# Bias rows of a two-layer transformer kernel written by GpSimd, entry by entry, instead of by three matmuls

## The chip, the cores and the metric

One NeuronCore of one Trainium2 chip. The metric is the device time of one execution in microseconds, the median of several. Engines are named as in the profile: PE is TensorE (its matmuls; PEld its weight loads), DVE is VectorE, ACT is ScalarE, POOL is GpSimd, SP is SyncE. A name with q behind it is that engine's queue of DMA issues.

## The reference

Two transformer blocks on one sequence of 512 tokens and 16 meta tokens, width 1024. What matters here is the first block's position bias. A table `rel_bias` of 32 buckets by 16 heads holds it: the first 8 columns serve attention A (a sliding window), the last 8 attention B (top-k latent attention). The bias of a query and a key depends on their distance alone:

```python
def t5_bucket(dist):
    max_exact = N_BUCKETS // 2
    d = jnp.maximum(dist, 1).astype(jnp.float32)
    large = max_exact + (jnp.log(d / max_exact) / math.log(MAX_DISTANCE / max_exact)
                         * (N_BUCKETS - max_exact)).astype(jnp.int32)
    large = jnp.minimum(large, N_BUCKETS - 1)
    return jnp.where(dist < max_exact, dist, large)
...
    bias = bias_table[t5_bucket(jnp.maximum(dist, 0))]
    s = jnp.where(allowed[None, :, None, None], s + bias.astype(jnp.float32)[None], NEG)
```

Around it stand the input product with `w_in` (1024 to several thousand columns, cut into queries, keys, values and gates), the two attentions, their output products, a gated feed-forward of width 2816, and then a second block of the same size.

## The kernel before

The kernel is written engine by engine: each engine has its own program, and semaphores join them. The order on each engine is the order in which its program is written; no scheduler moves anything. Weights come in slices of 1024 rows by 128 columns through two buffers, b = 0 and 1. For each slice SP issues the load into `stage` (`load`, L589), ACT rounds it to the high half `wh` (L918), DVE or POOL subtracts to get the low half `wl` (L1398 on DVE), and PE runs `product` (L2273): three matmuls for each 128 rows, of which the first waits for `lo[b]` (the low half is there) and for `ev[b]` (the result before it on this buffer has been taken out of PSUM). DVE takes results out, for the keys by `take_keys` (L1549), which multiplies them by `Rk`, the spread inverse norm of each token.

The change lies in the first 50 us. There the phases follow one another as `kv1` (four slices, in pairs 0 and 1: keys and values of both attentions), `bq1` (two slices), `iq1` (two), `aq1` (four). At that place the kernel before does this:

- SP loads the table into `tab` (33 partitions, one a bucket, the last a row of -1e30 set by POOL at L719) and two tables of zeros and ones, `hotA` (33 by 383) and `hotB` (33 by 655), which say for each distance which bucket it falls into (L633 to L635).
- PE, after pair 0 of `kv1`, spreads the inverse norms (`spread_first`, L2433: a small matmul for the meta tokens and one of 512 columns, L2365), then multiplies `tab` by the tables (L2443 to L2445). The results are two rows for each of 8 heads, the bias by distance. They lie in `psL` and `psT`. Then it goes on with pair 1 of `kv1`.
- ACT takes the spread norms out into `Rk` (L976), and DVE takes the meta part (L1522, L1523). When both are there, DVE takes out pair 0 (`bkvT`, `ikwT`), runs a dozen small operations (`start_rest`, L1526), copies the bias rows from PSUM into `fA` and `fB` (L1541 to L1544), and then makes the low half of pair 1's second slice.
- POOL waits for `fA_ok`, writes the two rows to DRAM (L786, L787), fans row A out to 128 copies in DRAM (L777), and reads them back, each partition one element further on, as the bias tile `biasA` (L783). Then it waits for `key_taken` (L792) and goes on with other work. Row B follows the same way much later, inside the loop of the gates (L796 to L801). The scores of attention A use `biasA` at L1697.

`fA` and `fB` lie in the same memory as the input tile `xin`.

Of the kernel before, what the change touches and what calls it, by code (L numbers as in the profile page):

```python
# [29 lines left out]
P = 128  # L30
# [4 lines left out]
NB = SEQ // P  # L35
# [8 lines left out]
NH = 8  # L44
EPS = 1e-6
NEG = -1e30
# [3 lines left out]
BUCKETS = 32  # L50
# [14 lines left out]
def bucket(dist):  # L65

    exact = BUCKETS // 2
    d = np.maximum(dist, 1).astype(np.float32)
    span = np.float32(np.log(128 / exact))
    large = exact + (np.log(d / np.float32(exact)) / span * np.float32(BUCKETS - exact)).astype(np.int32)  # L70
    return np.where(dist < exact, dist, np.minimum(large, BUCKETS - 1))


# [228 lines left out]
def build(nc, t, out):  # L302
    with ExitStack() as ctx:
# [8 lines left out]
        def at(name, shape, offset, dt=F32):  # L312

            n = int(np.prod(shape[1:])) * size[dt]
            assert offset + n <= nc.sbuf_usable_end, (name, offset + n - nc.sbuf_usable_end)
            return nc.alloc_sbuf_tensor_at(name, shape, dt, offset=offset), -(-(offset + n) // 32) * 32

        def keep(name, shape, dt=F32):
            tensor, top[0] = at(name, shape, top[0], dt)
            return tensor  # L320
# [18 lines left out]
        nsink = keep("nsink", [P, 2, NH])  # L339
        tab = keep("tab", [BUCKETS + 1, 2 * NH])  # L340
        wuv = keep("wuv", [P, NH * HD])
# [85 lines left out]
        sqacc, _ = at("sqacc", [P, 2, SEQ], tail)  # L427
        hotA, o5 = at("hotA", [BUCKETS + 1, LEN_A], tail)
        hotB, o5 = at("hotB", [BUCKETS + 1, LEN_B], o5)
        assert o5 <= o  # L430
        fA, o7 = at("fA", [NH, LEN_A], gate0)
# [85 lines left out]
        def last_bank(half, b):  # L517
# [27 lines left out]
            sem(n) for n in "consts zeros gvec_t gvec_ok x_t x_high xT_act xT_dve xlo x_sq meta_t metaT_ok mhi mlo".split()]  # L545
        f_mm, fA_ok, f_row, f_out, biasA_in, biasB_in = [sem(n) for n in "f_mm fA_ok f_row f_out biasA_in biasB_in".split()]
        diag_ok, bcast, R_ok, ssq_in, ssq_mm = [
# [40 lines left out]
        def _(sp):  # L588
# [43 lines left out]
            load("kv1", 0, 1, win1, kv_cols[1])  # L632
            sp.dma_start(tab[0:BUCKETS, :], t["rel_bias"]).then_inc(tab_in, 16)  # L633
            sp.dma_start(hotA[:], t["hot_a"]).then_inc(tab_in, 16)
            sp.dma_start(hotB[:], t["hot_b"]).then_inc(tab_in, 16)  # L635
            for n in range(2, 4):
# [71 lines left out]
        def _(pool):  # L708
# [9 lines left out]
                                        pattern=[[META, NH]], channel_multiplier=-1))  # L718
            own.link(pool.memset(tab[BUCKETS:BUCKETS + 1, :], NEG))  # L719
            own.link(pool.memset(st[:, 0, 0:6], 1.0))  # L720
# [58 lines left out]
            def windows(dram, length, tile_, width, h0, h1, signal):  # L779
# [3 lines left out]
                pool.dma_start(tile_[:, h0:h1, :], src).then_inc(signal, 16)  # L783

            pool.wait_ge(fA_ok, 2)
            pool.dma_start(fA_row[:], fA[:]).then_inc(f_row, 16)  # L786
# [598 lines left out]
        def _(v):  # L1385
# [140 lines left out]
            def start_rest():  # L1526

                b0 = ROW["b_gates"]
                g = ROW["subln_gain_2"]
                dv.link(v.tensor_scalar(subg[:], gvec[:, g:g + 1], 1.0 - LAMBDA0, None, ALU.mult))  # L1530
                g1, g2 = ROW["final_norm_g"], ROW["norm_mix_2"]
                dv.link(v.tensor_tensor(g12[:], gvec[:, g1:g1 + KD], gvec[:, g2:g2 + KD], ALU.mult))
                dv.link(v.tensor_scalar(bhalf[:], gvec[:, b0:b0 + 2 * KD], 0.5, None, ALU.mult))
                v.wait_ge(lam_in, 64)
                dv.link(v.tensor_tensor_reduce(out=lamj[:], in0=lam4[:, 0, :], in1=lam4[:, 1, :], scale=1.0, scalar=0.0,
                                               op0=ALU.mult, op1=ALU.add, accum_out=lam[:, 0:1]))
                dv.link(v.tensor_tensor_reduce(out=lamj[:], in0=lam4[:, 2, :], in1=lam4[:, 3, :], scale=1.0, scalar=0.0,
                                               op0=ALU.mult, op1=ALU.add, accum_out=lam[:, 1:2]))
                v.memset(lamj[:, 0:1], 0.0).then_inc(lam_sum, 1)
                v.wait_ge(f_mm, 1)  # L1540
                v.tensor_copy(fA[:], psL[0:NH, 0, 0:LEN_A]).then_inc(fA_ok, 1)  # L1541
                v.wait_ge(f_mm, 2)
                v.tensor_copy(fB[:, 0:512], psL[0:NH, 1, :])
                v.tensor_copy(fB[:, 512:LEN_B], psT[0:NH, 0, 0:LEN_B - 512]).then_inc(fA_ok, 1)  # L1544

# [726 lines left out]
        def _(pe):  # L2272
# [167 lines left out]
            spread_first()  # L2440
            pe.wait_ge(tab_in, 48)
            pe.wait_ge(xT_act, 6)
            pe.matmul(psL[0:NH, 0, 0:LEN_A], tab[:, 0:NH], hotA[:], start=True, stop=True).then_inc(f_mm, 1)  # L2443
            pe.matmul(psL[0:NH, 1, :], tab[:, NH:2 * NH], hotB[:, 0:512], start=True, stop=True)
            pe.matmul(psT[0:NH, 0, 0:LEN_B - 512], tab[:, NH:2 * NH], hotB[:, 512:LEN_B], start=True, stop=True).then_inc(f_mm, 1)  # L2445
            products("kv1", hn, first=1, meta=1)
            pe.wait_ge(fA_ok, 2)
            products("bq1", hn)
# [476 lines left out]
```

## Time and profile before

| | us |
|---|---|
| median of 3 runs | 1473.24 |
| lowest and highest | 1470.36, 1475.11 |
| profiled execution | 1473.38 |
| its span in the trace | 1471.7 |

The profiled execution takes 1.7 us more than its span, for what lies around it. The span begins at 0.00 in all the rows below. Mean granted clock of PE: 0.997 of full speed.

A row of the timeline gives start, duration, engine, line, operation, output and inputs; in square brackets stands the time for which the engine had been idle and who released it. A group of instructions that run into one another shows them as one row with their count, from the first start to the last end.

### The profile page before, as it was taken

The page shows a single profiled execution, that of the slowest core. Times are in us where ns is not written, and L with a number is a line of the kernel's source. Part 1 is how long each engine was busy: PE and PEld are TensorE (multiplying, and loading weights), DVE is VectorE, ACT ScalarE, POOL GpSimd, SP SyncE. Part 2 cuts the span into 40 slices and gives each one's busy share as a digit, 9 for nine tenths or more (in the row PEclk, how much of TensorE's full clock was granted, in tenths as well). Part 3 has the DMA queues.
Part 4 walks back from the last instruction along what each step waited for, and adds up shares of the span by engine and source line. Part 5 has one row for each costly group of instructions (what it writes and reads, how often), then busy time and mean ns, then how long its engine had stood idle before and what let it go on. Part 6 is the DMA issues. An engine that isn't in the chain of part 4 may idle for free.

```text
span 1471.7 us, 23871 instructions
## 1 busy us (share of the span) xinstructions
PE 1452.7 (99%) x8712; PEld 1253.2 (85%) x8712; DVE 975.2 (66%) x1779; ACT 654.3 (44%) x1175; POOL 258.2 (18%) x260
## 2 busy tenths in 40 slices
PE   9999999999999999999999999999999999999998
PEld 8868786888898898999899777777888988989997
DVE  6678977575776576787744372434767765867875
ACT  5234446535453353465411373544344533534643
POOL 2024536201101100000003675331011001000000
PEclk9999999999999999999999999999999999999999
DMA  7536674249899993663223237653388999736632
GB/s 187 148 100 211 173 133 130 79 111 191 202 328 226 250 217 98 199 184 106 86 86 86 58 101 162 151 188 80 107 186 226 305 218 242 213 95 195 185 104 93
DMA packets 342909, 236.91 MB, mean 161 GB/s; under 512 B 24729, under 2 KB 322837, under 8 KB 342814
## 3 DMA queue, kind: packets, MB, share of 16 engines
q1 hardware_dynamic: 305518, 152.24, 36.4%
q0 software_dynamic: 37216, 83.27, 24.8%
q8 instruction: 60, 0.98, 0.3%
q14 instruction: 35, 0.29, 0.1%
q10 hardware_dynamic: 80, 0.14, 0.0%
HBM read 233.48 MB, written 81.88 MB: 214 GB/s over the span
## 4 chain that ended last, share of the span: by engine, by line
PE 88%; DMA 6%; DVE 3%; ACT 1%; issue 1%; DVEq 0%; SPq 0%; POOL 0%; ACTq 0%
PE psL L2293 37%; PE psL L2520 12%; PE psS L2316 10%; PE psL L2316 6%; PE psS L2293 5%; PE psT L2316 4%; PE psT L2529 2%; DMA stage<-in_w_ffn_up 1%; DMA stage<-in_w_ffn_gate 1%; DMA stage<-in_w_ff_up 1%; PE psL L2655 1%; PE psS L2836 1%; PE psS L2570 1%; PE psL L2791 1%; PE psS L2814 1%
## 5 line engine op out<-in xcount | busy, mean ns | idle before, releaser
L918 ACT ACTIVATE wh<-stage 128x1024 fp32r<-128x1024 f32 (+3 forms) x211 | 203.6, 965 | 362.1 <-PE psL L2293 199.6
L1398 DVE TENSOR_TENSOR wl<-stage,wh 128x1024 fp32r<-128x1024 f32 (+2 forms) x168 | 183.8, 1094 | 57.7 <-ACT wh L918 57.3
L2293 PE MATMUL psL<-hid,wh 128*128 128x512 f32 x672 | 207.3, 390 | 0.0
L2520 PE MATMUL psL<-hn,wh 128*128 128x512 f32 x496 | 165.0, 414 | 0.8 <-DVE yn L2176 0.8
L2293 PE MATMUL psL<-hn,wh 128*128 128x512 f32 x528 | 165.0, 394 | 0.0
L2293 PEld LDWEIGHTS psL<-hid,wh 128*128 128x128 f32 x672 | 125.6, 188 | 26.2 <-DVE wl L1398 0.6
L2293 PE MATMUL psL<-hid,wl 128*128 128x512 f32 x336 | 130.7, 389 | 0.0
L746 POOL TENSOR_TENSOR wl<-stage,wh 128x1024 fp32r<-128x1024 f32 (+1 forms) x43 | 97.7, 2273 | 172.7 <-ACT wh L918 172.7
L2293 PEld LDWEIGHTS psL<-hn,wh 128*128 128x128 f32 x528 | 97.7, 188 | 23.1 <-issue 3.3
L2520 PEld LDWEIGHTS psL<-hn,wh 128*128 128x128 f32 x496 | 84.5, 189 | 24.5 <-issue 11.1
L2293 PE MATMUL psL<-hn,wl 128*128 128x512 f32 x264 | 102.9, 390 | 0.0
L1901 DVE TENSOR_TENSOR wsl<-wsum,wsh 128x1024 fp32r<-128x1024 f32 x72 | 88.2, 1224 | 22.3 <-ACT wsh L1166 21.4
L2520 PE MATMUL psL<-hn,wl 128*128 128x512 f32 x248 | 97.8, 394 | 0.0
L2316 PE MATMUL psS<-xt,wsh 128*128 128x256 f32 x432 | 80.2, 283 | 0.8 <-ACT part_x L1226 0.8
L2293 PE MATMUL psL<-mix,wh 128*128 128x512 f32 x256 | 79.9, 393 | 0.8 <-DVE wl L1814 0.8
L2293 PE MATMUL psS<-hn,wh 128*128 128x264 f32 x416 | 78.5, 290 | 0.9 <-DVE hn L1845 0.5
L1166 ACT ACTIVATE wsh<-wsum 128x1024 fp32r<-128x1024 f32 x72 | 75.4, 1048 | 5.6 <-DMA wsum<-weight_sums_1g 1.9
L2293 PEld LDWEIGHTS psL<-hid,wl 128*128 128x128 f32 x336 | 63.1, 188 | 13.2
L2028 DVE TENSOR_TENSOR ft<-psL,Rk 128x512 f32<-128x512 f32 x46 | 31.8, 691 | 62.4 <-PE psL L2293 62.4
L2316 PEld LDWEIGHTS psS<-xt,wsh 128*128 128x128 f32 x432 | 67.4, 192 | 1.0 <-ACT part_x L1226 1.0
L2293 PEld LDWEIGHTS psS<-hn,wh 128*128 128x128 f32 x416 | 65.7, 192 | 2.6 <-issue 1.2
L2316 PE MATMUL psS<-xt,wsl 128*128 128x256 f32 x216 | 61.1, 283 | 0.0
(507 smaller groups left out, 3333.0 us busy)
## 6 DMA issues: line engine op xcount, KB each, us to landing
stage<-in_w_in SPq DMA_DIRECT2D x53, 512.0 KB, 4.0
wsum<-weight_sums_1g SPq DMA_DIRECT2D x18, 512.0 KB, 5.2
wsum<-weight_sums_1u SPq DMA_DIRECT2D x18, 512.0 KB, 5.3
wsum<-weight_sums_2g SPq DMA_DIRECT2D x18, 512.0 KB, 4.7
wsum<-weight_sums_2u SPq DMA_DIRECT2D x18, 512.0 KB, 4.5
stage<-in_w_out SPq DMA_DIRECT2D x16, 512.0 KB, 4.7
stage<-in_w_ffn_down SPq DMA_DIRECT2D x32, 256.0 KB, 3.0
stage<-in_w_ff_down SPq DMA_DIRECT2D x32, 256.0 KB, 3.0
```

Source lines behind the costliest of these rows:

```text
L746: pool.tensor_tensor(wl[:, b, 0:n], stage[:, b, 0:n], wh[:, b, 0:n].bitcast(F32), ALU.subtract).then_inc(lo[b], 1)
L918: act.activation(wh[:, b, 0:n], stage[:, b, 0:n], ACT.Copy).then_inc(hi[b], 1)
L1166: act.activation(wsh[:, cols], wsum[:, cols], ACT.Copy).then_inc(ws_hi, 1)
L1398: v.tensor_tensor(wl[:, b, 0:n], stage[:, b, 0:n], wh[:, b, 0:n].bitcast(F32), ALU.subtract).then_inc(lo[b], 1)
L1901: v.tensor_tensor(wsl[:, cols], wsum[:, cols], wsh[:, cols].bitcast(F32), ALU.subtract).then_inc(ws_lo, 1)
L2028: v.tensor_tensor(ft[:, 2 * b, :], psL[:, b, :], R, ALU.mult).then_inc(upper_ok, 1)
L2293: ins = pe.matmul(dst, w[:, b, k * P:(k + 1) * P], x[:, part, k, c0:c1], start=done_ + n == 0, stop=done_ == kc - 1 and n == 2)
L2316: ins = pe.matmul(dst, w[:, cols], x(part, k), start=not add and k + n == 0, stop=k == KD // 2 - 1 and n == 2, skip_group_check=True)
L2520: ins = pe.matmul(psL[:, b, :], w[:, b, k * P:(k + 1) * P], hn[:, part_, k, META:], start=k + n == 0, stop=k == KD - 1 and n == 2)
L2529: ins = pe.transpose(psT[:, n % 2, m * P:(m + 1) * P], tile[:, col:col + P], ident[:])
L2570: ins = pe.matmul(psS[:, 2 * (i % 2) + 1, h * HD:(h + 1) * HD], PTa[:, u % 2, n * P:(n + 1) * P], avn[:, c, h // 4 * HD:h // 4 * HD + HD], ...
L2655: ins = pe.matmul(psL[:, i % 2, h * HD:(h + 1) * HD], PT[:, n % 4, m * P:(m + 1) * P], vB[:, c, h * HD:(h + 1) * HD], start=h == 0 and m = ...
```

## The change

The three matmuls, the two tables of zeros and ones, the row of -1e30 in `tab`, DVE's three copies and the semaphore `f_mm` go. The table is now loaded with heads on partitions (`tabT`, 8 partitions by 2 by 32), by two DMAs of SP that read it element by element. POOL writes `fA` and `fB` itself: for each run of distances with one bucket, a copy of that bucket's entry, broadcast over the run (`bucket_runs`); where no key is allowed, a memset to -1e30. Row A has 34 runs, 32 of them copies, and row B 33, also with 32 copies. Of these 64 copies 63 are of 1 to 15 elements and one is of 415. The third new thing is POOL's three waits ahead of them: for the table, for the squares of x and for DVE's `diag_ok`, since `fA` lies on `xin`. PE no longer waits for `fA_ok` ahead of `bq1`.

```diff
+def bucket_runs(length, far):
+
+    dist = (length - P) - np.arange(length)
+    which = np.where((dist < 0) | (dist >= far), BUCKETS, bucket(dist))
+    edges = [0, *(np.flatnonzero(np.diff(which)) + 1).tolist(), length]
+    return [(int(which[x0]), x0, x1) for x0, x1 in zip(edges[:-1], edges[1:])]
...
-        tab = keep("tab", [BUCKETS + 1, 2 * NH])
+        tabT = keep("tabT", [NH, 2, BUCKETS])
...
-            sp.dma_start(tab[0:BUCKETS, :], t["rel_bias"]).then_inc(tab_in, 16)
-            sp.dma_start(hotA[:], t["hot_a"]).then_inc(tab_in, 16)
-            sp.dma_start(hotB[:], t["hot_b"]).then_inc(tab_in, 16)
+            for n in range(2):
+                sp.dma_start(tabT[:, n, :], t["rel_bias"][:, n * NH:(n + 1) * NH].rearrange("b h -> h b"), allow_slow_non_contiguous=True).then_inc(tab_in, 16)
...
-            own.link(pool.memset(tab[BUCKETS:BUCKETS + 1, :], NEG))
...
+            pool.wait_ge(tab_in, 32)
+            pool.wait_ge(x_sq, NB - 1)
+            pool.wait_ge(diag_ok, 1)
+            for n, (row, length, far) in enumerate(((fA, LEN_A, P), (fB, LEN_B, 1 << 20))):
+                for b, x0, x1 in bucket_runs(length, far):
+                    if b == BUCKETS:
+                        ins = pool.memset(row[:, x0:x1], NEG)
+                    else:
+                        ins = pool.tensor_copy(row[:, x0:x1], tabT[:, n, b:b + 1].broadcast_to([NH, x1 - x0]))
+                ins.then_inc(fA_ok, 1)
             pool.wait_ge(fA_ok, 2)
...
-                v.wait_ge(f_mm, 1)
-                v.tensor_copy(fA[:], psL[0:NH, 0, 0:LEN_A]).then_inc(fA_ok, 1)
-                v.wait_ge(f_mm, 2)
-                v.tensor_copy(fB[:, 0:512], psL[0:NH, 1, :])
-                v.tensor_copy(fB[:, 512:LEN_B], psT[0:NH, 0, 0:LEN_B - 512]).then_inc(fA_ok, 1)
...
-            pe.wait_ge(tab_in, 48)
             pe.wait_ge(xT_act, 6)
-            pe.matmul(psL[0:NH, 0, 0:LEN_A], tab[:, 0:NH], hotA[:], start=True, stop=True).then_inc(f_mm, 1)
-            pe.matmul(psL[0:NH, 1, :], tab[:, NH:2 * NH], hotB[:, 0:512], start=True, stop=True)
-            pe.matmul(psT[0:NH, 0, 0:LEN_B - 512], tab[:, NH:2 * NH], hotB[:, 512:LEN_B], start=True, stop=True).then_inc(f_mm, 1)
             products("kv1", hn, first=1, meta=1)
-            pe.wait_ge(fA_ok, 2)
             products("bq1", hn)
```

How the order moves. On PE, between pair 0 and pair 1 of `kv1`, in the kernel before:

```order
L2436 MATMUL psS<-meta_diag,ones 128x32
L2365 MATMUL psT<-diag,ones 128x512
L2443 MATMUL psL<-hotA,tab 8x383
L2444 MATMUL psL<-hotB,tab 8x512
L2445 MATMUL psT<-hotB,tab 8x143
L2293 MATMUL psS<-hn,wh 128x264 x2
L2293 MATMUL psS<-hn,wl 128x264
```

and in the changed kernel (its lines are numbered some 8 higher there):

```order
L2301 MATMUL psS<-hn,wl 128x264
L2444 MATMUL psS<-meta_diag,ones 128x32
L2373 MATMUL psT<-diag,ones 128x512
L2301 MATMUL psS<-hn,wh 128x264 x2
L2301 MATMUL psS<-hn,wl 128x264
```

Pair 1 now stands right behind the spreading of the norms, with nothing between them. On POOL, behind its loads of the small vectors (`lam_86` holds the four lambda vectors), before:

```order
L739 DMA lam_86<-in_lambda_k_2 128x64
L786 DMA bias_row_A<-fA 8x383
L787 DMA bias_row_B<-fB 8x655
L777 DMA bias_by_distance_A<-bias_row_A 1024x1x383
L783 DMA biasA<-bias_by_distance_A 128x8x256
```

and in the changed kernel, where the copies of one element close row A:

```order
L794 MEMSET fA 8x128
L796 COPY fA<-tabT 8x15
L796 COPY fA<-tabT 8x14
...
L796 COPY fA<-tabT 8x1 x16
L794 MEMSET fA 8x127
L796 COPY fB<-tabT 8x415
...
L796 COPY fB<-tabT 8x1 x16
L794 MEMSET fB 8x127
L799 DMA bias_row_A<-fA 8x383
L800 DMA bias_row_B<-fB 8x655
```

67 instructions now stand ahead of the first of POOL's bias DMAs, on the engine that issues them.

## Rows read from the trace of the kernel before

**Rows 1.** The page: busy times; the engines of the chain that ended last.
```profile
PE 1452.7 (99%) x8712; PEld 1253.2 (85%) x8712; DVE 975.2 (66%) x1779; ACT 654.3 (44%) x1175; POOL 258.2 (18%) x260
...
PE 88%; DMA 6%; DVE 3%; ACT 1%; issue 1%; DVEq 0%; SPq 0%; POOL 0%; ACTq 0%
```

**Rows 2.** That chain in order of time: start us, us, what.
```profile
25.43 0.74 PE psL L2443 x2
26.16 0.86 PE psL L2444 x2
27.02 0.24 PE psT L2445 x2
27.27 11.78 PE psS L2293 x96
```

**Rows 3.** Timeline at the place of the change: PE, DVE, ACT.
```profile
27.20 0.51 PE L2293 MATMUL psS<-hn,wh 128*128 128x264 f32 x2
...
23.57 1.20 DVE L1398 TENSOR_TENSOR wl<-stage,wh 128x1024 fp32r<-128x1024 f32 x1
...
26.15 0.71 DVE L1549 TENSOR_TENSOR bkvT<-psS,Rk 128x528 f32<-128x528 f32 x1 [0.41 <-DVE Rmeta L1523]
...
28.55 0.54 DVE L1541 COPY fA<-psL 8x383 f32<-8x383 f32 x1
...
29.84 1.20 DVE L1398 TENSOR_TENSOR wl<-stage,wh 128x1024 fp32r<-128x1024 f32 x1
...
25.46 0.60 ACT L976 ACTIVATE Rk<-psT 128x512 f32<-128x512 f32 x1 [3.96 <-PE psT L2365]
...
50.06 1.06 ACT L918 ACTIVATE wh<-stage 128x1024 fp32r<-128x1024 f32 x1 [4.39 <-PE psL L2293]
```

**Rows 4.** POOL's instructions by line and form: count, busy us, mean ns, idle before.
```profile
L852 POOL COPY m8d<-W 128x16 f32<-128x16 f32 x16 | 3.2, 201 | 16.6 <-DVE W L2168 16.4
...
L861 POOL COPY vm<-vaT 128x512 f32<-128x512 f32 x1 | 1.0, 997 | 34.2 <-DVE vaT L1549 34.2
...
L713 POOL MEMSET lam_mask<- 128x1 f32 x1 | 0.1, 99 | 0.1
```

**Rows 5.** Timeline of POOL: its bias DMAs and what follows.
```profile
30.20 0.54 POOL L786 DMA_DIRECT2D bias_row_A<-fA  x1 [13.28 <-DVE fB L1544]
...
43.14 0.94 POOL L783 DMA_DIRECT2D biasA<-bias_by_distance_A  x1 [9.38 <-DMA bias_by_distance_A<-bias_row_A]
...
77.52 0.29 POOL L793 COPY cm<-cT 128x128 f32<-128x128 f32 x1 [33.44 <-DVE ikz L1624]
```

**Rows 6.** The tile biasA: its user (ns, first and last start), its landing.
```profile
L1697 DVE CUSTOM_DVE_ANT_0 W3a<-psS,biasA,nsink x32: 364/480/485, 107.8 to 209.7; 128x256 f32<-128x256 f32 x24, 128x144 f32<-128x144 f32 x8
...
DMA to landing us min/median/max: 6.0/6.0/6.0
```

**Rows 7.** SP's loads issued at 11.09 and 35.70 (KB, us to landing), and at 41.49.
```profile
stage<-in_w_in SPq DMA_DIRECT2D x1, 512.0 KB, 5.2
...
stage<-in_w_in SPq DMA_DIRECT2D x1, 512.0 KB, 8.6
...
41.49 0.37 SPq L595 DMA_DIRECT2D stage<-in_w_in  x1
```

**Rows 8.** DMA packets, MB, share of 16 engines: windows 54:57, then 16:20.
```profile
q1 hardware_dynamic: 1884, 0.47, 70.9%
...
q0 software_dynamic: 141, 0.15, 103.3%
```

**Rows 9.** PE's longest wait, and 516:520: engines' busy us, PEclk, DMA share, GB/s.
```profile
516.33 0.72 PE L2316 MATMUL psL<-xt,wsh 128*128 128x256 f32 x2 [2.23 <-ACT part_x L1226]
...
516.00:520.00 4.00, 3.67 (x18) 3.68 (x19) 3.90 (x5) 2.80 (x7) 0.00 (x0) 0.57 1.04 175
```

**Rows 10.** Timeline of DVE and POOL side by side in the second layer.
```profile
790.43 2.43 DVE L2113 TENSOR_SCALAR tmp<-dist 128x384 f32<-128x384 f32 x1
...
789.88 2.76 POOL L746 TENSOR_TENSOR wl<-stage,wh 128x1024 fp32r<-128x1024 f32 x1 [3.40 <-ACT wh L918]
```

More of the change, by code:

```diff
@@ L427, in build @@
         sqacc, _ = at("sqacc", [P, 2, SEQ], tail)
-        hotA, o5 = at("hotA", [BUCKETS + 1, LEN_A], tail)
-        hotB, o5 = at("hotB", [BUCKETS + 1, LEN_B], o5)
-        assert o5 <= o
         fA, o7 = at("fA", [NH, LEN_A], gate0)
@@ L545, in build @@
             sem(n) for n in "consts zeros gvec_t gvec_ok x_t x_high xT_act xT_dve xlo x_sq meta_t metaT_ok mhi mlo".split()]
-        f_mm, fA_ok, f_row, f_out, biasA_in, biasB_in = [sem(n) for n in "f_mm fA_ok f_row f_out biasA_in biasB_in".split()]
+        fA_ok, f_row, f_out, biasA_in, biasB_in = [sem(n) for n in "fA_ok f_row f_out biasA_in biasB_in".split()]
         diag_ok, bcast, R_ok, ssq_in, ssq_mm = [
```

## The prediction

> **What bounds the kernel now.** I read the page first: PE is busy for 99% of the span, and 88% of the chain that ended last is PE's [rows 1]. So an edit is worth what it takes off PE, or what it makes PE wait. Then I read that chain in order of time around 25 us, to see whether the removed matmuls are links of it. They are: 0.74, 0.86 and 0.24 us stand between the spreading of the norms and pair 1 of `kv1` [rows 2]. Third comes the timeline of the other engines at the same place, to see what PE would wait for if it came there earlier, and last POOL's idle time and the loads, for what the new work could push.
>
> **Removed from PE: 1.84 us, of which 0.3 count.** The three matmuls are 0.74 + 0.86 + 0.24 = 1.84 us of the chain [rows 2]. Without them PE is ready for pair 1 at 25.43. But the first slice of pair 1 writes the PSUM bank that `bkvT` is taken from (`ev[0]` in `product`), and `bkvT` is on DVE from 26.15 to 26.86 [rows 3]. It can't be earlier: it needs `Rk` from ACT, 25.46 to 26.06, and that is released by the spreading matmul [rows 3], which keeps its time. So the matmuls ran under a chain PE, ACT, DVE that is nearly as long as they are. PE starts pair 1 some 0.05 us behind DVE's end, at 26.91, where it started at 27.20 [rows 3]: 0.29 us gained, and some 1.5 us of new idle time. The other input of that slice, its low half, is ready at 23.57 + 1.20 = 24.77 [rows 3], before that. The price is bounded by 0, if DVE is held up by a few tenths, and by the whole 1.84. I take 0.29, because the row that sets it stands unchanged.
>
> **Removed from DVE: nothing on the path.** The three copies fill 28.55 to 29.84. Behind them waits the low half of pair 1's second slice, ready at 29.84 + 1.20 = 31.04 [rows 3]. PE's two slices of pair 1 are 11.78 us together [rows 2], so it comes to the second at 27.27 + 5.89 = 33.16. There were 2.1 us of slack. Now the low half is ready at 28.55 + 1.20 = 29.75 and PE comes at 32.9: 3.1 us. The wait of `bq1` for `fA_ok` was met at 30.1, long before PE came to it at 39.05, the end of pair 1 [rows 2]; its removal is worth nothing.
>
> **Added to POOL: 67 instructions, some 11 us, hidden.** They can start when DVE's `diag` is done, about where the next instruction begins, 23.57 [rows 3]. The trace has no copy of 8 partitions by 1 to 15. The nearest is one of 16 elements with 201 ns, and the cheapest POOL instruction of all is a memset with 99 ns [rows 4]. The copy of 512 elements takes 997 ns [rows 4], so 415 elements are 201 + (415 - 16) x (997 - 201) / (512 - 16) = 841 ns. With 63 short copies and three memsets the ends are 66 x 0.099 + 0.84 = 7.4 us and 66 x 0.201 + 0.84 = 14.1 us. I take 0.15 each, between the two, since instructions that run into one another overlap a little: 66 x 0.15 + 0.84 = 10.7 us. The rows are ready at 34.3 (31.0 to 37.7). POOL issued the first bias DMA at 30.20 [rows 5], so the chain of bias A moves back by 4.1 us (0.8 to 7.5). It ended with an issue at 43.14 [rows 5] and a landing 6.0 later, at 49.1, and its user starts at 107.8 [rows 6]. Now it ends at 53.2 (at most 56.6). POOL's next work is at 77.52 [rows 5], 33.4 us behind its last issue. Both covers hold unless each of the 66 costs over 0.6 us, three times the dearest row.
>
> **Moved: the big DMAs of bias A.** The fan-out to DRAM lay between 33 and 43 and moves to some 37 to 47; it is behind no queue of SP's, but it shares the 16 DMA engines. The load of a weight slice issued at 35.70 ran beside it and took 8.6 us [rows 7]. That load now gets shorter. The next, at 41.49 [rows 7], gets into it: at 8.6 us it lands at 49.8 after an issue at 41.2. ACT rounds that slice at 50.06 [rows 3], at 49.8 in the changed kernel. So it lands just in time. PE wants the slice only behind `iq1`'s first product, seven us later. Cost: 0, at most a few tenths on ACT that PE never sees.
>
> **Added to SP: 512 single elements in place of three small tables.** The table now comes in 2 x 8 x 32 runs of 4 bytes, on the same queue ahead of the load issued at 11.09, which landed at 11.09 + 5.2 = 16.3 [rows 7]. The nearest hardware-made small packets are 1884 of 256 bytes, which filled 0.709 x 16 x 3 us = 34 us of engine time, 18 ns each [rows 8]. The dear end is a stretch of software-made ones, reading short vectors again and again: 1.033 x 16 x 4 = 66 us for 0.15 MB, that is 590 runs of 256 bytes at 0.11 us [rows 8]. Spread over all 16 engines, 32 runs each, they delay the load by 0.6 to 3.6 us; on 8 of them, a head each, by 1.2 to 7.2. The load may land so late that rounding (1.06) and low half (1.20) [rows 3] still end by 25.5, when DVE turns to `Rk`: until 23.2, a delay of 6.9 us. I take 1.2 us and a cost of 0, with some 0.3 us at the dear end. The table itself is needed only at 23.6.
>
> The last rows show no number of engines. The Trainium skill says (DMA: Bandwidth & Descriptors, "Why a DMA increments its semaphore by 16 and not by 1") that a copy runs on the largest count up to 16 that divides the slowest dimension of both sides, here 8, and (same page, "Rules for kernel authors") that a strided last dimension becomes one descriptor per element. It warns against this load; by it 64 elements lie on each of 8 engines, still inside the slack. No row here shows the split.
>
> **The sum.** -0.29 (PE) + 0 (DVE) + 0 (POOL) + 0 (DMAs) = -0.3 us. The profiled execution took 1473.38 (its span 1471.7 and 1.7 around it), so 1473.1 for it; on the median of 1473.24 it gives 1473.0. A measurement of this kernel can tell some 0.3%, 4.4 us, from no change.
>
> **Rivals.**
> 1. *PE's clock falls in the new gap: slower.* PE's longest wait in the trace, 2.23 us, is followed by 4 us with a mean granted clock of 0.57 [rows 9]: full speed before, half speed (1.2 instead of 2.4 GHz) in most of them, and 4 x 0.43 = 1.7 us lost. The new gap is 1.5 us, in a stretch where PE is otherwise full. It would give -0.3 + 1.7 = +1.4: 1474.6. For it speaks that the gap is of that order, against it that it is a third shorter. The point from which it decides lies at or under 2.2 us.
> 2. *POOL's stream holds DVE up: slower.* In the second layer a DVE instruction of 384 columns took 2.43 us, which began beside a POOL instruction already running; POOL's ended at 789.88 + 2.76 = 792.64 and DVE's at 792.86 [rows 10]: it waited for POOL's to end. Now 66 POOL instructions stand in a row from 23.6 to 34.3, and DVE's low half of the second slice falls among them at 28.6. If DVE gets in between two of them, each of its ten or so instructions loses at most 0.2 us, 2.0 together, within the 3.1 of slack. If it doesn't, the low half starts at 34.3 and ends at 35.5, PE waits 2.6 us (6.0 at the dear end of POOL), and the sum is +2.3 to +5.7: 1475.5 to 1479. It decides when DVE loses over 3.1 us. Against it: in [rows 10] one POOL instruction's end was enough.
> 3. *All of 1.84 is gained: faster.* That needs `bkvT` out at 25.5, before its norms are there. 1471.4. Only if the rows of ACT and DVE there move as well, for which I see no reason.
> 4. *The single elements hold the queue: slower.* If all 512 go through one engine, they take 9 us at 18 ns, and the load lands at 25.5. Rounding and low half then end at 27.8, with `Rk` behind them on both engines, and PE starts at about 28.6: +1.4, and at 0.11 us a run, +46. It decides from 6.9 us of delay.
> 5. *Nothing of it reaches the time.* The 0.29 is lost to tenths on DVE: 1473.2. The change does remove the matmuls, so it does what it says.
>
> By the Trainium skill (SBUF — State Buffer, "SBUF: two separate sides") DVE and GpSimd share a port pair as an exclusive lock for the whole instruction, the loser blocked. That agrees with the 2.43 us above, and it is why rival 2 has a chance at all; whether a waiting DVE is served between two POOL instructions no row shows beyond the one.
>
> **How the numbers follow.** Forecast (0.1 to 0.6 us gained) 0.60; rival 5 0.08; rival 1 0.14; rival 2 0.09; rival 3 0.04; rival 4 0.05. Predicted: 1473.0. Forecast and rivals 1, 3 and 5 span 1471.4 to 1474.6, and the runs of the kernel before lie 2.9 below and 1.9 above their median. Rival 2 reaches to 1479. I give 1470.3 to 1476.3, which takes in the cheap half of rival 2 and leaves out its dear half, rival 4 and the tails of the runs. Faster by over 4.4 us: 0.02, for no case reaches it but by the spread of runs. Slower by over 4.4 us: 0.06, the dear ends of rivals 2 and 4. Within: 0.92.
>
> **What would show it.** Right: PE's row behind the spreading has an idle time of about 1.5 us that ends on DVE's `bkvT`, and pair 1 starts 0.3 us earlier; POOL's small copies start at 23.6 to 24.8, take 0.1 to 0.2 us each, and its first bias DMA is at 31 to 38; `biasA` has landed by 57; PE waits for no low half before 60 us. Rival 1 shows as a granted clock under 1 between 25 and 32 us, rival 2 as a wait of PE for L1398 near 33 us, rival 4 as ACT waiting for a load near 20 us. A wait of POOL for the table, or a time outside 1470 to 1476 without one of these, would make the prediction wrong.

## The result: 1.0% slower, and the profile after

| | before | after |
|---|---|---|
| median, us (runs) | 1472.23 (6) | 1487.47 (6) |
| lowest and highest | 1467.59, 1475.11 | 1482.78, 1490.24 |
| profiled execution | 1473.38 | 1488.68 |
| its span | 1471.7 | 1486.9 |

The ratio of after to before is 1.0103, with a 95% interval of 1.0079 to 1.0127. The forecast was 1473.0 in a range of 1470.3 to 1476.3; the kernel takes 15 us more. The prediction was wrong.

The page of after, busy times, and engines of the chain that ended last, to be held against [rows 1]:

```profile
PE 1466.0 (99%) x8706; PEld 1252.4 (84%) x8706; DVE 974.3 (66%) x1776; ACT 654.3 (44%) x1175; POOL 268.3 (18%) x326
...
PE 91%; DMA 4%; DVE 3%; ACT 1%; issue 1%; DVEq 0%; POOL 0%; SPq 0%; ACTq 0%
```

PE has six matmul records fewer (three instructions, each recorded twice) and is busy for 13.3 us more. DVE and ACT stand where they stood. Outside its busy time PE has 20.9 us of the span, where it had 19.0, and 1.6 of that are the new gap. So the loss is no wait: the same matmuls take longer. The place of the change shows nothing of the kind. The chain of after in order of time (start us, us, what), to be held against [rows 2]:

```profile
26.70 1.07 PE psT L2373 x2
28.48 0.72 DVE bkvT L1557
29.34 11.91 PE psS L2301 x96
41.25 11.21 PE psL L2301 x48
54.10 11.21 PE psL L2301 x48
```

Between the end of the spreading, 27.77, and pair 1 at 29.34 lie 1.57 us, where 1.84 us of matmuls stood: 0.27 gained. But the last two rows have counterparts in the chain of before:

```profile
39.05 10.92 PE psL L2293 x48
...
51.60 10.93 PE psL L2293 x48
```

These are two products with the same 48 matmuls of 512 columns each, and there is no wait in them. They take 11.21 instead of 10.92 us: 233.5 ns a matmul instead of 227.5, 2.6% more, at a granted clock of 1.00 in both (the window of after is shown below). All rows of after here stand some 2 us later than those of before. That is scatter of the start: pair 0 of `kv1` begins at 20.88 in this trace, at 18.55 in that of before, and at 18.4 to 22.4 in those of the kernels below, whatever they change.

The groups of PE in the whole program, by form (count | busy us, mean ns | idle before), before:

```profile
L2293 PE MATMUL psL<-hid,wh 128*128 128x512 f32 x672 | 207.3, 390 | 0.0
L2293 PE MATMUL psL<-hn,wh 128*128 128x512 f32 x528 | 165.0, 394 | 0.0
...
L2316 PE MATMUL psL<-hn,wh 128*128 128x256 f32 x288 | 53.4, 283 | 0.0
...
L2316 PE MATMUL psS<-hn,wsh 128*128 128x256 f32 x144 | 26.7, 283 | 0.0
```

and after:

```profile
L2301 PE MATMUL psL<-hid,wh 128*128 128x512 f32 x672 | 211.3, 396 | 0.0
L2301 PE MATMUL psL<-hn,wh 128*128 128x512 f32 x528 | 167.9, 399 | 0.0
...
L2324 PE MATMUL psL<-hn,wh 128*128 128x256 f32 x288 | 52.5, 281 | 0.0
```

Nearly every large group of 512 columns has grown (summed over all of them, +15.7 us; one, the gates' matmuls with `wl`, stands at 97.8), and those of 256 columns with `wh` and `wl` have shrunk a little (all groups of 256 columns together -3.7 us). The two sum to 12.0 of the 13.3 us. The rest is +1.6 on the products of 264 columns, +2.1 on the transposes of `xin` and `metain` in the first 16 us, and -2.2 for the matmuls removed. The change edits none of the matmuls that have grown or shrunk. What they share is that their operands have moved: the diff in front replaces `tab`, 64 bytes on each partition, by `tabT`, 256 bytes, in a list of tiles that are laid one behind the other. Everything behind it lies 192 bytes further on: `hn`, `xt` (at `gate0`), `oA` and `oB` (on `hn`), `mix` and `hid` (at `ar0`), and the split weights `wsh` and `wsl` of the feed-forward. `stage` and the weight tiles `wh` and `wl` lie ahead of it and stay.

### The profile page after: what moved, and what is told of

The parts are those of the page before. It is cut to its first block, busy times and chain, and to the rows that moved or that the text cites. A ratio compares the mean times of both kernels' runs of the same rounds, so it can differ in the third digit from the quotient of the medians.

```text
span 1486.9 us, 23921 instructions
## 1 busy us (share of the span) xinstructions
PE 1466.0 (99%) x8706; PEld 1252.4 (84%) x8706; DVE 974.3 (66%) x1776; ACT 654.3 (44%) x1175; POOL 268.3 (18%) x326
## 4 chain that ended last, share of the span: by engine, by line
PE 91%; DMA 4%; DVE 3%; ACT 1%; issue 1%; DVEq 0%; POOL 0%; SPq 0%; ACTq 0%
PE psL L2301 40%; PE psL L2523 12%; PE psS L2324 9%; PE psL L2324 6%; PE psS L2301 5%; PE psT L2324 5%; PE psT L2532 2%; DMA wsum<-weight_sums_2u 1%; DMA stage<-in_w_ffn_up 1%; PE psL L2658 1%; PE psS L2839 1%; PE psS L2573 1%; PE psL L2794 1%; PE psS L2817 1%; PE psS L2631 1%
## 5 line engine op out<-in xcount | busy, mean ns | idle before, releaser
L1411 DVE TENSOR_TENSOR wl<-stage,wh 128x1024 fp32r<-128x1024 f32 (+2 forms) x168 | 184.0, 1095 | 53.7 <-ACT wh L931 53.2
L2301 PE MATMUL psL<-hid,wh 128*128 128x512 f32 x672 | 211.3, 396 | 0.0
L2301 PE MATMUL psL<-hn,wh 128*128 128x512 f32 x528 | 167.9, 399 | 0.0
L2523 PE MATMUL psL<-hn,wh 128*128 128x512 f32 x496 | 166.8, 417 | 0.8 <-DVE yn L2184 0.8
L2301 PEld LDWEIGHTS psL<-hn,wh 128*128 128x128 f32 x528 | 97.8, 188 | 25.6 <-issue 3.1
L2523 PE MATMUL psL<-hn,wl 128*128 128x512 f32 x248 | 97.8, 394 | 0.0
L1179 ACT ACTIVATE wsh<-wsum 128x1024 fp32r<-128x1024 f32 x72 | 75.5, 1049 | 10.3 <-DMA wsum<-weight_sums_2u 7.2
```

Source lines behind the costliest of these rows:

```text
L1179: act.activation(wsh[:, cols], wsum[:, cols], ACT.Copy).then_inc(ws_hi, 1)
L1411: v.tensor_tensor(wl[:, b, 0:n], stage[:, b, 0:n], wh[:, b, 0:n].bitcast(F32), ALU.subtract).then_inc(lo[b], 1)
L2301: ins = pe.matmul(dst, w[:, b, k * P:(k + 1) * P], x[:, part, k, c0:c1], start=done_ + n == 0, stop=done_ == kc - 1 and n == 2)
L2523: ins = pe.matmul(psL[:, b, :], w[:, b, k * P:(k + 1) * P], hn[:, part_, k, META:], start=k + n == 0, stop=k == KD - 1 and n == 2)
```

## The experiments

The theory from here on: the spacing of the matmuls follows where the moving operand lies against the weights, and nothing else of the change costs. The rivals: the new work at the start costs the 15 us in some way that its own rows don't show; or what counts is the address itself, or one of the moved tiles that isn't an operand of PE. "Distance" below is the start of the moving tile less that of the weights, counted from what it is in the kernel before. There all the tiles named above start at multiples of 256 bytes, and their rows follow one another in steps of such multiples, so a tile's matmuls of 512 or 256 columns all have one distance, up to multiples of 256. Each kernel was timed beside the kernel before on the same chip.

### 1. The changed kernel with its tiles where they were

```diff
-        tabT = keep("tabT", [NH, 2, BUCKETS])
+        keep("gap", [P, 2 * NH])
...
         sqacc, _ = at("sqacc", [P, 2, SEQ], tail)
+        tabT, _ = at("tabT", [NH, 2, BUCKETS], tail)
```

The gap is as large as `tab` was, and the table lies in memory that is free in the first 50 us.

> The changed kernel, with tabT moved to memory that is free at that time, and a 64-byte gap where tab was, so that every tile behind it has the address that it had in the kernel before. Theory A (the 192 bytes by which the change moved all later tiles slow PE's 512-column matmuls from 227 to 233 ns start to start): 1472 us, matmuls of hid at 227 ns. Theory B (the work itself costs it: POOL's copies, the element-wise load, the gap on PE, or PE's shorter program): still 1487 us and 233 ns.

Median 1470.87 us (1465.71 to 1473.98), ratio 1.0004 [0.9988, 1.002]. Its page, its 512-column groups and its chain:

```profile
PE 1451.2 (99%) x8706; PEld 1252.6 (85%) x8706; DVE 974.9 (66%) x1776; ACT 654.0 (44%) x1175; POOL 268.2 (18%) x326
...
L2302 PE MATMUL psL<-hid,wh 128*128 128x512 f32 x672 | 207.3, 390 | 0.0
L2302 PE MATMUL psL<-hn,wh 128*128 128x512 f32 x528 | 165.1, 394 | 0.0
...
40.63 10.92 PE psL L2302 x48
```

This is what theory A said. POOL's stream, the loads of single elements, the gap on PE: all of the change is in this kernel, and the loss is gone. The groups are those of before.

### 2 and 3. The kernel before with its tiles moved

One line behind `tab`, with 192 and with 128 bytes:

```diff
         tab = keep("tab", [BUCKETS + 1, 2 * NH])
+        top[0] += 192
```

> The kernel before, with 192 unused bytes behind tab: no instruction changes, all later tiles have the addresses of the changed kernel. Theory A: 1487 us, 512-column matmuls 233 ns apart. Theory B: 1472 us.

> The kernel before with 128 unused bytes behind tab. Within theory A: if what counts is a multiple of 256 bytes, about 1487 us like plus 192; if a multiple of 128 is enough, 1472. Theory B: 1472.

192 bytes: 1487.64 us, ratio 1.0104 [1.0054, 1.0154], PE busy for 1469.1 us. That is the whole loss of the change (1.0103) without any of its instructions. 128 bytes: 1484.07 us, 1.0075 [1.004, 1.0109]. Both are near what theory A said, for 128 bytes the first of its two values. The two runs together with the first show the cause of the result from both sides.

### 4 and 8. How far: 64 and 32 bytes

The same line with `+= 64` and `+= 32`.

> The kernel before with 64 unused bytes behind tab. Within theory A: if a multiple of 64 bytes were enough, the changed kernel would not have been slow, so about 1487 us; a smaller loss would say that the distance to the boundary counts. Theory B: 1472.

> The kernel before with 32 unused bytes behind tab. If the spacing of the 512-column matmuls rises step by step with the distance (227 at 0, 229 at 64, 232.5 at 128, 233.4 at 192): 227 to 229 ns and 1470 us. If 32 bytes break a smaller boundary that all of 0, 64, 128 and 192 keep: over 234 ns and over 1488 us.

64 bytes: 1469.96 us, 1.0003 [0.9987, 1.0019]. 32 bytes: 1484.79 us, 1.0082 [1.0049, 1.0114]. Both came out otherwise than expected: with 64 bytes a loss was expected, with 32 either none or a larger one than with 192. So more isn't worse, and the loss isn't that a multiple of 256 is left: 32, 128 and 192 cost 0.8 to 1.0%, 64 nothing. The groups of the kernel with 64 show that a loss and a gain meet:

```profile
L2294 PE MATMUL psL<-hid,wh 128*128 128x512 f32 x672 | 207.9, 390 | 0.0
L2294 PE MATMUL psL<-hn,wh 128*128 128x512 f32 x528 | 166.2, 396 | 0.0
...
L2317 PE MATMUL psL<-hn,wh 128*128 128x256 f32 x288 | 50.7, 276 | 0.0
...
L2317 PE MATMUL psS<-hn,wsh 128*128 128x256 f32 x144 | 26.7, 283 | 0.0
...
39.66 11.00 PE psL L2294 x48
```

The 512-column products pay a little (11.00 against 10.92), while the 256-column matmuls with `wh` have gained: 50.7 against 53.4 us. Those with `wsh` haven't. `wsh` moved along with `hn`, `wh` didn't. Over all groups it is +5.2 us with 512 columns and -12.6 with 256, and PE is busy for 5.3 us less in this trace. The median shows less of it, 0.5 us; the profiled execution (1465.92) is the fastest of its ten.

### 5. Distance or address

```diff
-        base = -(-nc.sbuf_base // 256) * 256
+        base = -(-nc.sbuf_base // 256) * 256 + 192
```

Now everything moves by 192 bytes, the weights too.

> The kernel before with every tile, the weights' wh and wl too, moved up by 192 bytes. If the address itself counts (PE's moving operand or its weights off a multiple of 256 bytes): 1487 us or more, 512-column matmuls at 233 ns or more. If only the distance between moving operand and weights counts (two reads of PE that meet in memory): 1471 us and 227 ns, since all distances are as before.

1476.7 us, 1.0037 [1.0018, 1.0057]. Its page, groups and chain:

```profile
PE 1453.7 (99%) x8712; PEld 1252.5 (85%) x8712; DVE 976.1 (66%) x1779; ACT 653.2 (44%) x1175; POOL 257.9 (18%) x260
...
L2293 PE MATMUL psL<-hn,wh 128*128 128x512 f32 x528 | 165.2, 394 | 0.0
...
39.65 10.92 PE psL L2293 x48
```

The time lies between the two that were expected, 1471 and 1487. PE's products are those of before (each large group within 0.5 us), so for them it is the distance and not the address. The median is nonetheless 5 us above that of before, which PE's busy time (+1.0) doesn't explain. What moved here and in no other kernel is all that lies ahead of the table: `stage`, where the DMAs of the weights land, `wh`, `wl`, `hT`, `Rk` and smaller tiles. The landings of the small slices are a little longer, 3.4 and 3.3 us in the median where they were 3.0. The DMAs of SP's queue filled 37.4% of the 16 engines' time, 36.4% with the same packets and bytes in the kernel before, and 35.8 to 36.6% in all other kernels here. And PE waits 1.3 us for low halves (L1398) at products where it had no such wait. So late weights are the nearest explanation, but no run moves the landing place alone, and the profiled execution is only 2.0 us longer than that of before: it stays open.

### 6 and 7. One group of tiles at a time

The first moves `hid`, `mix`, `wsum`, `wsh` and `wsl` by 192 bytes in the kernel before and leaves `hn`, `xt`, `oA` and `oB`; the second, made from the first experiment, moves `hn`, `xt`, `oA` and `oB` back by 192 bytes and leaves the others:

```diff
-        ar0 = top[0]
+        ar0 = top[0] + 192
```

```diff
-        tabT = keep("tabT", [NH, 2, BUCKETS])
...
-        Rmeta = keep("Rmeta", [P, 2, META])
...
         hn_rows = keep("hn", [P, 2, KD, HN_ROW], F32R)
+        Rmeta = keep("Rmeta", [P, 2, META])
+        keep("gap", [P, 2 * NH])
```

> The kernel before with only the region of hid and mix (and what shares it: ft, wsum, wsh, wsl) moved up by 192 bytes; hn, oA, oB, xt and the weights stay. If it is each tile's own address: hid 233.4 and mix 233.3 ns apart as in the changed kernel, hn, oA and oB at 227 to 229 as before; 1003 x 6.5 + 382 x 5.7 ns = 8.7 us, so 1479 us. If it is something common to the program: all slow together or none.

> The changed kernel with tabT out of the way as in e1, and Rmeta and the 64-byte gap moved behind hn: gate, xt, hn, oA and oB start 64 bytes behind a multiple of 256, hid and mix on one. With the spacings that plus 64 and plus 0 showed for each tile: hn 256 columns 1188 x -4.3 ns = -5.1 us, xt 256 columns 1602 x -2.5 = -4.0, hn 512 columns 1398 x +0.9 = +1.3, oA and oB 352 x +1.8 = +0.6: 7 us less than the kernel before, 1464 us. If the gain at 256 columns came from wsh and wsl (they don't move here), xt gains nothing: 1467.

The first: 1470.83 us, 0.9988 [0.9969, 1.0007]. The second: 1469.15 us, 0.9986 [0.9964, 1.0007]. Groups of the first:

```profile
L2293 PE MATMUL psL<-hid,wh 128*128 128x512 f32 x672 | 211.3, 396 | 0.0
...
L2293 PE MATMUL psL<-hn,wh 128*128 128x512 f32 x528 | 165.0, 394 | 0.0
...
L2316 PE MATMUL psS<-hn,wsh 128*128 128x256 f32 x144 | 25.4, 276 | 0.0
```

Of the matmuls of 512 columns only those with the moved tiles are slower, `hid` here and `mix` (81.0 against 79.9 us); those with `hn` and `wh` are untouched. And the 256-column matmuls with `wsh` have gained, where `hn` stood still and the weights moved. So each pair of tiles has its own price. The 1479 us expected were missed for that reason: the sum had the 8.7 us lost on `hid` and `mix` and not the gain with `wsh` and `wsl`, 15.5 us over their groups. The second run missed both of its values, 1464 and 1467. It gave less than a distance of +64 did, though -192 is the same in steps of 256: both sets of 256-column matmuls lie between (52.3 and 26.1 us). `hn` and `xt` are at -192 to both sets of weights there, and 9 and 12 show that this is what matters.

### 9 and 10. Put to use

If the matmuls with `hid` and `mix` are fastest at a distance of 0 and the 256-column ones at +64, each can have its own. The ninth kernel gives both sets of weights +64:

```diff
         tab = keep("tab", [BUCKETS + 1, 2 * NH])
+        top[0] += 64
...
-        mix, o = at("mix", [P, 2, KD, SEQ], ar0, F32R)
+        mix, o = at("mix", [P, 2, KD, SEQ], ar0 + 192, F32R)
...
-        hid, o = at("hid", [P, 2, NFH, SEQ], ar0, F32R)
+        hid, o = at("hid", [P, 2, NFH, SEQ], ar0 + 192, F32R)
...
-        part_z, o = at("part_z", [P, SEQ], o)
-        sums0 = o
+        sums0 = tail - 64 - 3 * 4 * 4 * SEQ
...
-        inner2, _ = at("inner2", [P, SEQ], o)
+        inner2, o = at("inner2", [P, SEQ], o)
+        part_z, _ = at("part_z", [P, SEQ], o)
```

The tenth has the last two pieces alone: `part_z` goes elsewhere, and `wsum`, `wsh` and `wsl` begin 64 bytes earlier.

> The kernel before with three groups of tiles placed by their distance to the weights: hn and xt 64 bytes further on (with all that lies behind the table's tile), hid and mix 256 bytes further on than before, wsum, wsh and wsl back at the address of before, for which part_z goes to the free place behind inner2. Nothing is left out. If the distance between moving operand and weights alone sets the spacing, the 512-column matmuls of hid and mix keep 227 to 229 ns a start, those of hn and oA/oB have 229 to 230, and every 256-column one (with wh and with wsh) falls from 120 to 113 or 114: by the groups of the runs before some 10 us less with wh and 15 us less with wsh and wsl, 3 us lost on hn and oA/oB. PE's busy time 1429 to 1434 us, median 1448 to 1456. If the gain is only in how the records are modelled, or turns into waits for ACT and DVE at the split weights, PE's groups show it but the median stays at 1466 to 1471.

> The kernel before with wsum, wsh and wsl alone 64 bytes nearer to hid (part_z goes behind inner2 to make room); nothing else moves and nothing is left out. If a distance of +64 bytes is what the 256-column matmuls like, only those with wsh and wsl change: 120 to 113 or 114 ns a start, their groups 283 to 277 ns, some 15 us less PE time, median 1455 to 1461. If the distance counts in one direction only, or the waits for ACT's part_x take the gain, the median stays at 1466 to 1471.

The ninth: 1467.3 us, 0.9969 [0.9957, 0.9981]. The tenth: 1464.35 us, 0.996 [0.9947, 0.9973]. Both expectations were too high in gain; in the ninth PE is busy for 1450.7 us, not 1429 to 1434. The groups of the ninth, with `wh` and with `wsh`:

```profile
L2318 PE MATMUL psL<-hn,wh 128*128 128x256 f32 x288 | 52.4, 279 | 0.0
...
L2318 PE MATMUL psS<-hn,wsh 128*128 128x256 f32 x144 | 26.2, 279 | 0.0
```

In the ninth both are at +64, and neither has the 50.7 and 25.4 us that each had alone (4 and 6). The page, groups and waits (total us, times, longest) of the tenth:

```profile
PE 1440.6 (99%) x8712; PEld 1240.9 (85%) x8712; DVE 973.0 (67%) x1779; ACT 654.0 (45%) x1175; POOL 257.9 (18%) x260
...
L2317 PE MATMUL psL<-hn,wh 128*128 128x256 f32 x288 | 53.4, 283 | 0.0
...
L2317 PE MATMUL psS<-hn,wsh 128*128 128x256 f32 x144 | 25.4, 276 | 0.0
...
PE psL L2317 <- ACT part_x L1227: 6.5, 4, 3.4
```

PE is busy for 12.1 us less than before, nearly the 15 expected. The median fell by 7.0. In this trace 2.6 us of the difference are a longer wait for ACT's `part_x`; in the kernel before that wait is 3.9:

```profile
PE psL L2316 <- ACT part_x L1226: 3.9, 3, 2.2
```

The two profiled executions themselves are 10.3 us apart (1463.07 and 1473.38), so what is missing to the 7.0 of the medians lies between executions and not in a row: those of one kernel lie 4 to 13 us apart, and one profile against a median can't settle 3 us.

### 11 and 12. The change with the better place, and what the ninth lacked

The eleventh is the first kernel (the change, tiles back) with the edit of the tenth. The twelfth is the ninth with one number changed, so that `wsh` and `wsl` move along with `hn`:

```diff
-        sums0 = tail - 64 - 3 * 4 * 4 * SEQ
+        sums0 = tail - 3 * 4 * 4 * SEQ
```

> The changed kernel with both placements: the tiles behind the table back at the addresses of before, and wsum, wsh and wsl 64 bytes nearer to hid. Nothing is left out. If only the addresses made the loss and the change itself costs nothing, this is the same as the kernel before with that one placement: 1463 to 1466, ratio to before 0.994 to 0.998. If the change has a cost of its own that the first experiment hid in its spread, it stands at 1467 or more.

> As the ninth kernel (hn and xt 64 bytes further on, hid and mix 256 bytes), but with wsum, wsh and wsl 64 bytes further on too, so that only the products with wh and wl have the distance of +64. Nothing is left out. If it is the two sets of weights at the same distance that gave 117.5 ns there, the 256-column matmuls with wh now take 113.4 and those with wsh 120, as in the fourth kernel. If the place of hid or part_z did it, those with wh stay at 117.5. PE's busy time 1444 to 1448 in the first case; median 1464 to 1469.

The eleventh: 1465.49 us, 0.9965 [0.9951, 0.9978], PE busy for 1442.6 us. The change costs and brings nothing that can be told there either, as expected. The twelfth, as expected too: 1468.43 us, 0.9982 [0.9967, 0.9998], with these groups:

```profile
L2295 PE MATMUL psL<-hid,wh 128*128 128x512 f32 x672 | 207.3, 390 | 0.0
...
L2318 PE MATMUL psL<-hn,wh 128*128 128x256 f32 x288 | 50.7, 276 | 0.0
...
L2318 PE MATMUL psS<-hn,wsh 128*128 128x256 f32 x144 | 26.7, 283 | 0.0
```

As soon as `wsh` is off +64, the matmuls with `wh` have their full gain again. `hid`, `part_z` and `hn` lie as in the ninth, so none of them held it back. And `hid`, 256 bytes from its old place, has its 207.3 back: for it 256 is as good as 0. With -192 next to +64 in 6 and 10, all that was tried fits a distance counted in steps of 256.

The mean time from one matmul's start to the next, within a product, worked out from the records of each trace (ns; distances in bytes to `wh`, or for the last but one column to `wsh`):

| kernel | hid: distance, 512 cols | hn: distance, 512 cols | hn, wh: 256 cols | hn: distance, wsh: 256 cols | median us, ratio |
|---|---|---|---|---|---|
| before | 0, 226.9 | 0, 228.8 | 120 | 0, 120 | 1 |
| changed | +192, 233.3 | +192, 233.4 | 118 | 0, 120 | 1487.47, 1.0103 |
| 1 | 0, 226.9 | 0, 228.9 | 120 | 0, 120 | 1470.87, 1.0004 |
| 2 | +192, 233.4 | +192, 233.4 | 118 | 0, 120 | 1487.64, 1.0104 |
| 3 | +128, 232.6 | +128, 232.4 | 119 | 0, 119 | 1484.07, 1.0075 |
| 8 | +32, 233.3 | +32, 233.1 | 117 | 0, 120 | 1484.79, 1.0082 |
| 4 | +64, 228.9 | +64, 229.7 | 113.5 | 0, 120 | 1469.96, 1.0003 |
| 5 | 0, 227.0 | 0, 228.9 | 120 | 0, 120 | 1476.7, 1.0037 |
| 6 | +192, 233.3 | 0, 229.0 | 120 | -192, 113 | 1470.83, 0.9988 |
| 7 | 0, 227.0 | -192, 230.0 | 117 | -192, 117 | 1469.15, 0.9986 |
| 9 | +256, 227.0 | +64, 229.7 | 117.5 | +64, 117.5 | 1467.3, 0.9969 |
| 10 | 0, 226.9 | 0, 228.9 | 120 | +64, 113.5 | 1464.35, 0.996 |
| 11 | 0, 226.9 | 0, 228.9 | 120 | +64, 114 | 1465.49, 0.9965 |
| 12 | +256, 226.9 | +64, 229.7 | 113.5 | 0, 120 | 1468.43, 0.9982 |

## Why the prediction was wrong

**The step that failed** is a term of the sum that isn't there. The sum has PE's removed matmuls (-0.29) and 0 for DVE, POOL and the DMAs; the matmuls that the change doesn't touch were put at nothing, without a reason. They cost 12.0 us more in the trace of after, and experiment 2 gives the whole loss (1.0104) by the 192 bytes alone, without any of the change's instructions. The line that decides stood in the diff, a tile of 64 bytes replaced by one of 256 in the middle of a list. No rival had it either: all five were about the first 60 us, so the range could not hold it. The rows in front could not have given the price, since in the kernel before the large operands all lie at one distance. They do say how much hangs on it: PE is busy for 1452.7 us at 99% [rows 1], so 1% on its matmuls is 14.5 us of the time. A rival on what lies behind the new tile could have been named without its price.

**What held**, by rows of after. POOL (start, us, line, operation, idle time and its releaser), against [rows 5]:

```profile
25.67 0.19 POOL L794 MEMSET fA<- 8x128 f32 x1 [8.06 <-DVE diag L1463]
25.81 4.78 POOL L796 COPY fA<-tabT 8x15 f32<-8x15 f32 x32
30.54 0.19 POOL L794 MEMSET fA<- 8x127 f32 x1
30.69 5.33 POOL L796 COPY fB<-tabT 8x415 f32<-8x415 f32 x32
35.96 0.19 POOL L794 MEMSET fB<- 8x127 f32 x1
36.44 0.54 POOL L799 DMA_DIRECT2D bias_row_A<-fA  x1 [0.29 <-POOL fB L794]
...
49.13 0.94 POOL L786 DMA_DIRECT2D biasA<-bias_by_distance_A  x1 [9.13 <-DMA bias_by_distance_A<-bias_row_A]
```

- *POOL, 10.7 us of copies*: 10.5 (25.67 to 36.15). That it is so near is in part luck. By their records most short copies start 0.12 us apart, less than the 0.15 taken, and the one of 415 elements took 0.53 us, not 0.84; two short copies that ran beside a DVE instruction took 0.89 and 1.18 us and made up for it (see rival 2). The stream began on DVE's `diag`, as said, and waited for no table.
- *Bias A by 57*: the issue at 49.13 landed 6.3 us later, at 55.4; its first user starts at 111.0. The 4.1 us by which the chain was to move back are 49.13 - 43.14 = 6.0 in the traces, 2 of them the later start.
- *PE, 0.29 of 1.84 gained*: 1.84 - 1.57 = 0.27. The wait is there, and it ends on `bkvT`:

```profile
29.34 0.48 PE L2301 MATMUL psS<-hn,wh 128*128 128x264 f32 x2 [1.58 <-DVE bkvT L1557]
```

- *Rival 1, the clock*: in this trace full speed (2.4 GHz) behind the gap of 1.58 us, so it cost nothing more. Windows of after, the second inside the first of the two longer products; columns as in [rows 9]:

```profile
29.30:33.00 3.70, 3.66 (x30) 3.69 (x31) 2.82 (x10) 0.04 (x1) 3.70 (x20) 1.00 0.17 50
41.00:52.00 11.00, 11.00 (x50) 8.92 (x49) 3.85 (x4) 2.12 (x2) 0.94 (x1) 1.00 0.86 221
```

But rival 1 is not refuted. Four of the kernels have the gap (after, 1, 7 and 11), each with 1.58 us. In the traces of three the clock stays up behind it. In that of the eleventh it falls as pair 1 starts, to half speed (1.2 GHz) for most of 3.5 us, and pair 1 takes 13.39 us instead of 11.78 [rows 2]: the 1.7 us of rival 1, nearly. The first row is from its chain, the second its window:

```profile
30.14 13.39 PE psS L2303 x96
...
30.10:33.60 3.50, 3.46 (x16) 3.49 (x17) 2.93 (x10) 0.04 (x1) 3.50 (x18) 0.53 0.02 6
```

The same gap comes with both, so its length alone doesn't decide. One trace in four would be 0.4 us in the mean, an estimate from these four, and too little for the medians to show.

- *Rival 2, POOL's stream and DVE*: DVE's low half fell among the copies and was somewhat longer, 1.42 us against 1.20 [rows 3]. It was not held to the end of the stream, and PE waited for no low half. It got in between two copies, and the next one, of 14 elements, ended only with it (32.36 and 32.30 us):

```profile
30.88 1.42 DVE L1411 TENSOR_TENSOR wl<-stage,wh 128x1024 fp32r<-128x1024 f32 x1
...
31.18 1.18 POOL L796 COPY fB<-tabT 8x14 f32<-8x14 f32 x1
```

The traces of 1, 7 and 11 show the same: one short copy of 1.18 to 1.19 us that ends with DVE's low half, which takes 1.22 us there. So the cheap case of rival 2 holds, and the one that waits is mostly POOL.

- *Rival 4, single elements*: the load behind the table's was issued at 11.67 and landed in 4.1 us, where it took 5.2 before [rows 7]. (The dear end, 512 x 0.11 us, is 56 us and gives some +48 by the prediction's own working, not +46; nothing hangs on it.) ACT's rounding that the late load would have held up runs without an idle time ahead of it:

```profile
22.41 1.06 ACT L931 ACTIVATE wh<-stage 128x1024 fp32r<-128x1024 f32 x1
```

- *The sum of -0.3*, without the addresses: experiment 1 gives 1.0004 [0.9988, 1.002], that is +0.6 us and between -1.8 and +2.9. It can't tell -0.3 from 0 or from rival 1's +1.4, and it excludes rivals 2 and 4 at their dear ends.

So PE's gap and gain came out to a tenth, POOL's stream near its value by other parts, and the total was wrong by 15 us.

## What to carry to other kernels

A tile that is added, dropped or resized moves all that is laid out behind it; ahead of costing a change, list what lies behind it, and for a change meant to be neutral keep the old addresses with a gap or put the new tile last. Where PE is the bound, read the mean ns of the same matmul forms before and after first: if they differ throughout the program, look for what all of them share and not at the place of the change. And a layout is worth trying on its own: 64 bytes on `wsum`, `wsh` and `wsl` gave 0.4% here, where the change by itself gave nothing.

## What the runs showed of the hardware that was not expected

- The spacing of fp32 matmuls in this kernel depends on the distance between the start of the moving tile and that of its weights. With 512 columns: 227 ns at 0 and +256 bytes, 229 to 230 at +64 and -192, 232 to 233 at +32, +128 and +192. With 256 columns: 120 ns at 0, 113.5 at +64 and -192, 117 to 119 at +32, +128 and +192. Moving both tiles together leaves it as it is (experiment 5), moving either alone changes it (4 and 10). Why the distance counts no run shows. The Trainium skill (SBUF — State Buffer, "Operand start alignment") asks only for a start at a multiple of the element size, and says that this is about legality and that its runs timed nothing; here all starts are legal, and 6 ns in 227 hang on them.
- When the matmuls with `wh` and those with `wsh`, which follow one another in groups of 12 in the feed-forward, are both at +64 or both at -192, all of them take 117 to 118 ns (9 and 7); with one set off it, the other takes 113.5 (12 and 10). Both together gain no more than one alone. Why is open; no run separates it further.
- Moving the landing place of the weights and all else by 192 bytes costs 0.37% with PE's products unchanged (5). Open as well.
- GpSimd copies 8 partitions by 1 to 15 elements at one start every 0.12 us (the median of each of four traces) when the copies run into one another, each 0.17 to 0.19 us long.
- DVE's subtraction of one SBUF tile from another (L1411 in the changed kernel) was served between two copies of such a stream. In each of the four traces two copies met one, and lasted until 0.05 us behind its end: 0.89 to 0.90 and 1.18 to 1.19 us instead of 0.18. DVE itself took 1.42 instead of 1.20 us in one of them, where it started while the copy of 415 elements ran.
